# Sample keys turned by VectorE in 32x32 blocks, and scores in sixteen 32x32 tiles

## The chip, the cores and the metric

The kernel runs on one core of one Trainium2 chip. The metric is the device time of one launch in microseconds (us). The engines are TensorE (PE, with its weight loads as PEld), VectorE (DVE), ScalarE (ACT), GpSimd (POOL) and SyncE (SP); SP and POOL issue the DMAs named here.

## What is computed

Two layers of a decoder, for a prompt of 1024 tokens and for 8 sample sequences of 4 new tokens each; both share all weights. Layer 0 has a gated convolution and, beside it, differential attention. For the samples this attention reads 2048 past tokens per sequence from a paged cache: 16 pages of 128 tokens, each page a key page and a value page of 128 x 512 numbers (4 heads of 128, 256 KB in fp32), found through a page table. This is the part that the change touches:

```python
def diff_attend(q, k, v, mask, lam):
    s = jnp.einsum('bqhcd,bkhcd->bhcqk', q, k).astype(jnp.float32) * (DA_DIM ** -0.5)
    s = jnp.where(mask, s, -jnp.inf)
    p = jax.nn.softmax(s, axis=-1)
    w = p[:, :, 0] - lam * p[:, :, 1]
    return jnp.einsum('bhqk,bkhe->bqhe', w.astype(v.dtype), v)

past_k = cache_k[j, page_table].reshape(nb, -1, DA_HEADS, 2 * DA_DIM)
past_v = cache_v[j, page_table].reshape(nb, -1, DA_HEADS, 2 * DA_DIM)
keys = jnp.concatenate([past_k, k_rows], axis=1).reshape(b, p + s, DA_HEADS, 2, DA_DIM)
mask = jnp.arange(p + s)[None, :] <= (p + jnp.arange(s))[:, None]
attn = diff_attend(q, keys, vals, mask, lam)
```

The scores sum over the 64 numbers of a half head, so a key page has to stand with these numbers on the partitions, while it arrives from memory with the tokens on the partitions.

## The kernel before

Each engine has a program of its own, written out in order, and semaphores join them. Products of the large projections are made unit by unit: a unit is 24 fp16 matmuls of 128 x 352 into one PSUM bank (L372), then ACT or DVE copies the bank out. Three units share a weight tile (a visit); ACT and DVE split each weight tile into a high and a low fp16 half (L329, L345).

The attention heads of the prompt run first (`dve_head`, `pe_head`), and the units of the projection fill TensorE between their steps. In head 3 DVE also builds the sample queries: `dve_queries` clears row 19 of `arena` and makes 16 small copies, so that `q_blk` holds for each head and each sequence 32 columns, most of them zero.

Then comes the sample stage, in two rounds of four sequences. A round has four parts:

- keys: 64 key pages in 32 steps of two pages. TensorE turns both pages (8 transposes of 128 x 128, L1941) into banks 4 and 5, ACT copies bank 4 and DVE bank 5 to `kt` (L2010, L2070), and one step later TensorE makes the scores of these pages (`scores`, four matmuls of 128 x 32 by 256 columns, one for each head, side by side in the four 32-column strips of the array, L1929). The scores lie in banks 0 to 3. DVE takes the maximum of a bank as soon as it is full (`bank_max`, L2065);
- middle: the scores of the samples' own new tokens (L1952), the exponentials by ACT (L2016), their sums, and the weights turned and combined (L1958, L1960, L1965);
- values: 64 value pages in 32 steps of two (L1980), weights times values into bank 6;
- end: norm and copy-out of the result.

Both kinds of page pass through a ring of 16 pages in `hT` (`ring`). `load_page` (L1876) issues page f when page f - 16 has been used (`page_used`); SP issues two pages, then POOL the next two. The SP program also issues the weight tiles of the units (`sp_proj0`).

The order between sample work and units is written out: `woven` takes one step of the sample stage and then so many half units (12 matmuls) as ROUND_FILL has at this place. Before, it has none in the 32 key steps, two after each of the four middle steps, one in every second value step (15), and three in the end part: 26 half units a round, which is 13 units. DVE and ACT follow the same list; the second of a unit's two places is where the engine that copies the unit out waits for it. From the second convolution head on, all units use PSUM bank 7, so a unit starts when the one before it has been copied out. The units of a visit come in the order gate (copied by ACT, L1513), input (DVE, L1572) and output gate (DVE, L1591); with the first unit of the last kind DVE also makes the three convolution taps (L1538 to L1545).

After head 3 DVE still copies `v_own` (L2049), for which it waits until POOL has stored the prompt's keys and values.

Of the kernel before, what the change touches and what calls it, by code (L numbers as in the profile page):

```python
# [78 lines left out]
def build(nc, x_p, x_s, cache_k, cache_v, state_conv, state_C, state_n, state_m, page_table, norms, w_in0,  # L79
# [3 lines left out]
    with ctx:  # L83
# [1359 lines left out]
        sm_max, sm_neg = small[:, 80:85], small[:, 85:86]  # L1443
# [5 lines left out]
        q_blk = arena[:, 19, 0:SEQ].rearrange("p (h b n) -> p h b n", h=HEADS, b=NB)  # L1449
# [4 lines left out]
        kt = [arena[:, 24 + i, 0:SEQ].rearrange("p (h n) -> p h n", h=HEADS) for i in range(2)]  # L1454
# [24 lines left out]
        kp_ev = [sem("kp_ev0"), sem("kp_ev1")]  # L1479
        kp_used = sem("kp_used")  # L1480
        own_t, max_ready, exps, comb_ready = sem("own_t"), sem("max_ready"), sem("exps"), sem("comb_ready")
        q_ready, o_zero = sem("q_ready"), sem("o_zero")
# [38 lines left out]
        def dve_proj0(dve, chain, v0, v1_):  # L1521
# [24 lines left out]
            for n in range(VISITS[v0].units[0], VISITS[v1_].units[-1] + 1):  # L1546
                v, g, x = UNITS[n].visit, UNITS[n].g, ps[:, UNITS[n].bank, :]
                h, m = (v - CXB) // 3 if v >= CXB else v // 3, v % 3
                if v >= CXB and m == 2 and g == 0:
                    chain.sync()  # L1550
                    chain.mark(dve.tensor_copy(conv_new[:, h, 0:2], conv_p_in[:, SEQ:SEQ + 2]))
                    chain.mark(dve.tensor_copy(conv_new[:, h, 2:2 + 2 * NB].rearrange("p (b t) -> p b t", b=NB),
                                               conv_s_in[:, :, 4:6]))
                    tap(h, 0)
# [258 lines left out]
        def dve_head(dve, chain, h):  # L1813
# [19 lines left out]
            if h == HEADS - 1:  # L1833
                dve_queries(dve, chain)
# [20 lines left out]
        def dve_queries(dve, chain):  # L1855

            chain.link(dve.memset(arena[:, 19, 0:SEQ], 0.0))
            for b in range(NB):
                for c in range(2):
                    n = 8 * (b % 4) + 4 * c  # L1860
                    ins = dve.tensor_copy(q_blk[64 * c:64 * c + 64, :, b, n:n + NS],
                                          qT[64 * c:64 * c + 64, :, SEQ + NS * b:SEQ + NS * b + NS])
            ins.then_inc(q_ready, 1)

        ROUND_FILL = ((0,) * 32 + (2, 2, 2, 2) + (1, 0) * 15 + (0, 0) + (1, 1, 1))
# [40 lines left out]
        def pe_samples(pe):  # L1907
# [12 lines left out]
            pe.wait_ge(q_ready, 1)  # L1920
            for r_ in range(2):
                def scores(q):

                    n, b, j = 32 * r_ + q, 4 * r_ + q // 8, q % 8
                    pe.wait_ge(kp_ev[0], n + 1)
                    pe.wait_ge(kp_ev[1], n + 1)
                    pe.wait_ge(exps, 5 * r_)
                    for h in range(HEADS):
                        ins = pe.matmul(ps[32 * h:32 * h + 32, j // 2, 256 * (j % 2):256 * (j % 2) + 256],  # L1929
                                        q_blk[:, h, b, :], kt[n % 2][:, h, :], start=(b % 4 == 0 and j % 2 == 0),  # L1930
                                        stop=(b % 4 == 3), skip_group_check=True)
                    ins.then_inc(kp_used, 1)
                if r_:
                    pe.wait_ge(os_lo, 1)
                for q in range(32):
                    for e in range(2):
                        f = 128 * r_ + 2 * q + e
                        page_ready(f)
                        pe.wait_ge(kp_ev[e], 32 * r_ + q)
                        for h in range(HEADS):  # L1940
                            ins = pe.transpose(ps[:, 4 + e, h * P:(h + 1) * P], ring[:, f % RING, h * P:(h + 1) * P],  # L1941
                                               ident[:, :])
                        ins.then_inc(page_used, 1)
                    if q:
                        scores(q - 1)
                    yield
                scores(31)
# [51 lines left out]
        def act_samples(act):  # L1999
# [5 lines left out]
            for r_ in range(2):  # L2005
                for q in range(32):
                    n = 32 * r_ + q
                    act.wait_ge(page_used, 128 * r_ + 2 * q + 1)
                    act.wait_ge(kp_used, max(n - 1, 0))
                    act.activation(kt[n % 2][:, :, 0:P], ps[:, 4, :].rearrange("p (h e) -> p h e", h=HEADS),  # L2010
                                   ACT.Copy).then_inc(kp_ev[0], 1)
# [3 lines left out]
                for j in range(4):  # L2015
                    act.activation(probs[:, 512 * j:512 * j + 512], ps[:, j, :], ACT.Exp, bias=sm_neg,  # L2016
                                   accum_out=sm_sum[:, j:j + 1]).then_inc(exps, 1)
# [26 lines left out]
        def dve_samples(dve, chain):  # L2044
# [17 lines left out]
            for r_ in range(2):  # L2062
                def bank_max(j):
                    dve.wait_ge(kp_used, 32 * r_ + 26 + 2 * j)
                    chain.mark(dve.tensor_reduce(sm_max[:, j:j + 1], ps[:, j, :], AX.X, ALU.max))  # L2065
                for q in range(32):
                    n = 32 * r_ + q
# [733 lines left out]
        def _(pool):  # L2801
# [45 lines left out]
            for h in range(HEADS):  # L2847
                for ev, src, dst, n in ((v_ev, v_nat, v_p, 2), (k_ev, k_nat, k_p, 2)):
# [250 lines left out]
```

## Time and profile before

| | us |
|---|---|
| median of 3 runs | 2697.01 |
| the runs | 2692.72 to 2698.54 |
| span of the profiled execution | 2696.3 |
| PE busy in it | 2624.9 |
| DVE busy in it | 1245.7 |
| ACT busy in it | 1026.6 |
| POOL busy in it | 447.6 |

The profiled execution's span and the median differ by 0.7 us. Times in the rows below are counted from the start of the span. A row of the timeline merges instructions of one kind that follow each other; in brackets stands how long the engine was idle before and who ended it. Four records of fp32 matmul with 32-column weights lie on each other, since they use different strips of the array, so the time of one (mean ns) is much more than the time from one to the next. An fp32 matmul has two records. A row of the windows view gives the stretch and its length, then busy time and number of instructions of PE, PEld, DVE, ACT and POOL, the granted clock, the mean busy share of the DMA engines, and GB/s.

### The profile page before, as it was taken

Reading aid. Unit: us, or ns where it says so; the run is one execution under the profiler, and the core shown is the slowest. Engines: PE = TensorE matmul, PEld = TensorE weight load, DVE = VectorE, ACT = ScalarE, POOL = GpSimd, SP = SyncE. Lnnn points to the kernel's source line nnn. Section 1 sums busy time; section 2 is a strip of 40 time slices with the busy share of each in tenths; the row PEclk is TensorE's granted clock in tenths of the full one; section 3 lists DMA queues with packets and bytes.
Section 4 is the critical chain, followed back from the end, with each engine's and each line's share of the span. In section 5 each row is a group of like instructions: output and inputs, shape, how many; then the busy total and the mean of one; then the engine's idle time right before and its main releaser. Section 6 shows DMA issues by size and latency. Waiting matters only on the chain.

```text
span 2696.3 us, 49457 instructions
## 1 busy us (share of the span) xinstructions
PE 2624.9 (97%) x20217; PEld 1876.1 (70%) x20217; DVE 1245.7 (46%) x2059; ACT 1026.6 (38%) x1896; POOL 447.6 (17%) x512
## 2 busy tenths in 40 slices
PE   8999899999999999999999999999999999999998
PEld 5666666656588768886566766667656886788765
DVE  5555533335744213444754344344477541154454
ACT  4454332224443214333443333324365431244333
POOL 4000023222033002311101020111101220123121
PEclk9999999999999999999999999999999999999999
DMA  7211269771211311125435242322411112011442
GB/s 250 63 40 42 87 220 342 239 251 50 78 64 33 81 53 59 53 76 160 119 89 89 36 118 45 102 62 88 151 52 69 63 57 62 32 64 48 134 130 97
DMA packets 257659, 266.14 MB, mean 99 GB/s; under 512 B 10668, under 2 KB 217810, under 8 KB 256796
## 3 DMA queue, kind: packets, MB, share of 16 engines
q1 hardware_dynamic: 231772, 166.10, 22.0%
q0 software_dynamic: 25088, 94.79, 10.0%
q8 instruction: 162, 2.65, 0.4%
q10 hardware_dynamic: 576, 2.10, 0.2%
q14 instruction: 61, 0.50, 0.1%
HBM read 227.45 MB, written 35.50 MB: 98 GB/s over the span
## 4 chain that ended last, share of the span: by engine, by line
PE 90%; DVE 5%; ACT 2%; issue 1%; DMA 0%; POOL 0%; SPq 0%; DVEq 0%; ACTq 0%; POOLq 0%
PE ps L372 49%; PE ps L1130 25%; PE ps L1941 2%; PE ps L1929 1%; PE ps L1627 1%; PE ps L1980 1%; PE ps L1706 1%; PE ps L2475 1%; PE ps L2455 1%; PE ps L2489 1%; PE ps L2511 1%; DVE arena L883 1%; PE ps L2498 1%; PE ps L1692 1%; DVE hT L887 1%
## 5 line engine op out<-in xcount | busy, mean ns | idle before, releaser
L372 PE MATMUL ps<-u,w_split 128*128 128x352 f16 (+1 forms) x4752 | 753.0, 315 | 9.8 <-DVE u L737 5.9
L372 PEld LDWEIGHTS ps<-u,w_split 128*128 128x128 f16 (+1 forms) x4752 | 462.7, 99 | 260.8 <-issue 20.8
L372 PE MATMUL ps<-arena,w_split 128*128 128x352 f16 x3663 | 560.7, 313 | 3.7 <-DVE w_split L345 1.5
L372 PEld LDWEIGHTS ps<-arena,w_split 128*128 128x128 f16 x3663 | 357.6, 98 | 200.7 <-issue 9.4
L1130 PE MATMUL ps<-hT,w_split 128*128 128x264 f16 x3456 | 400.6, 276 | 3.2 <-ACT arena L1170 3.2
L1130 PEld LDWEIGHTS ps<-hT,w_split 128*128 128x128 f16 x3456 | 337.8, 98 | 54.9 <-issue 2.1
L345 DVE SCALAR_TENSOR_TENSOR w_split<-w_raw,w_split 128x1024 f16<-128x1024 f32 (+2 forms) x133 | 184.5, 1389 | 296.6 <-ACT w_split L329 296.1
L1130 PE MATMUL ps<-u,w_split 128*128 128x264 f16 x2592 | 303.4, 276 | 0.0
L1130 PEld LDWEIGHTS ps<-u,w_split 128*128 128x128 f16 x2592 | 253.6, 98 | 38.3
L329 ACT ACTIVATE w_split<-w_raw 128x1024 f16<-128x1024 f32 (+2 forms) x133 | 155.5, 1171 | 135.7 <-PE ps L372 97.3
L343 DVE SCALAR_TENSOR_TENSOR w_split<-arena,w_split 128x512 f16<-128x512 f32 x126 | 85.9, 724 | 103.9 <-ACT w_split L323 103.9
L1260 POOL TENSOR_TENSOR arena<-arena 128x512 f32<-128x512 f32 x18 | 22.8, 1266 | 527.6 <-DVE w_split L343 527.6
L343 DVE SCALAR_TENSOR_TENSOR w_split<-w_raw,w_split 128x512 f16<-128x512 f32 x126 | 80.9, 687 | 62.4 <-ACT w_split L323 62.4
L372 PE MATMUL ps<-arena 128*128 128x352 f16 x657 | 102.7, 316 | 0.0
L2325 ACT ACTIVATE arena<-ps 128x352 f32<-128x352 f32 x66 | 30.5, 464 | 179.7 <-PE ps L372 179.7
L817 POOL TENSOR_TENSOR arena<-arena 128x352 f32<-128x352 f32 x53 | 71.6, 1351 | 159.9 <-ACT arena L805 159.8
L1203 DVE TENSOR_TENSOR arena<-ps,arena 128x528 f32<-128x528 f32 x36 | 25.5, 707 | 153.4 <-ACT arena L1170 153.4
L1300 ACT ACTIVATE arena<-ps 128x352 f32<-128x352 f32 x48 | 22.3, 465 | 191.3 <-PE ps L372 191.3
L372 PEld LDWEIGHTS ps<-arena 128*128 128x128 f16 x657 | 64.5, 99 | 37.1 <-issue 3.1
L1216 DVE TENSOR_TENSOR arena<-arena 128x1056 f16<-128x1056 f32 (+1 forms) x60 | 58.3, 972 | 50.4 <-ACT arena L1153 41.4
L372 PE MATMUL ps<-u,arena 128*128 128x352 f16 x504 | 77.5, 313 | 3.2 <-ACT arena L1298 2.7
L323 ACT ACTIVATE w_split<-arena 128x512 f16<-128x512 f32 x126 | 71.8, 620 | 13.7 <-PE ps L1130 10.9
(405 smaller groups left out, 2987.1 us busy)
## 6 DMA issues: line engine op xcount, KB each, us to landing
w_raw<-in_w_down SPq DMA_DIRECT2D x58, 704.0 KB, 4.7
w_raw<-in_w_in SPq DMA_DIRECT2D x56, 512.0 KB, 7.7
arena<-in_w_gu SPq DMA_DIRECT2D x18, 1024.0 KB, 5.2
w_raw<-in_w_gu SPq DMA_DIRECT2D x18, 1024.0 KB, 5.2
hT<-in_cache_k SPq DMA_DIRECT2D x64, 256.0 KB, 4.3
hT<-in_cache_k POOLq DMA_DIRECT2D x64, 256.0 KB, 4.6
hT<-in_cache_v SPq DMA_DIRECT2D x64, 256.0 KB, 5.0
hT<-in_cache_v POOLq DMA_DIRECT2D x64, 256.0 KB, 5.5
```

Of the source, the lines that this page charges most:

```text
L323: act.activation(split_of(v, 0).rearrange("p (k n) -> p k n", k=kt), raw_of(v), ACT.Copy, scale=WS).then_inc(w_hi, 1)
L329: act.activation(split_of(v, 0)[:, 0:kt * n], raw_of(v), ACT.Copy, scale=WS).then_inc(w_hi, 1)
L343: dve.scalar_tensor_tensor(lo, raw_of(v), WS, hi, ALU.mult, ALU.subtract).then_inc(w_ready, 1)
L345: dve.scalar_tensor_tensor(split_of(v, 1)[:, 0:kt * n], raw_of(v), WS, split_of(v, 0)[:, 0:kt * n], ALU.mult, ALU.subtract).then_inc(w_rea ...
L372: ins = pe.matmul(ps[0:m, bank, 0:GW], split_of(v, wp)[:, k * w + col * P:k * w + col * P + m], x[:, xp, k0 + k, cols(g)], start=(k == 0 a ...
L817: pool.tensor_tensor(sum_y, sum_y, sq_y[k % 2], ALU.add).then_inc(y_added, 1)
L883: ins = dve.scalar_tensor_tensor(h_tmp[:, k % 2, :], ybuf[:, k, cols(g)], gains[:, col:col + 1], rs[0], ALU.mult, ALU.mult)
L887: dve.tensor_tensor(h, h, h_tmp, ALU.add).then_inc(h_ready, 1)
L1130: ins = pe.matmul(ps[:, bank + s_, 0:HW], split_of(v, wp)[:, k * P:(k + 1) * P], x, start=(name in ("M1", "M2", "M5") and k == 0 and q == ...
L1216: dve.tensor_tensor(hi_lo[:, 1], x, hi_lo[:, 0], ALU.subtract).then_inc(hid_ready, 1)
L1941: ins = pe.transpose(ps[:, 4 + e, h * P:(h + 1) * P], ring[:, f % RING, h * P:(h + 1) * P], ident[:, :])
L2325: act.activation((q_of[h % 2], k1, v1, o1)[m // 2][:, m % 2, cols(g)], ps[:, UNITS[n].bank, 0:GW], ACT.Sigmoid if m >= 6 else ACT.Copy, sc ...
```

## The change

- TensorE no longer turns key pages. DVE turns them where they lie in the ring, two pages (128 x 1024) with one instruction, in blocks of 32 x 32 (`dve.transpose`), and signals `page_turned`. Block (i, j) of a page keeps its place and is transposed inside, so each 32-partition strip holds 32 tokens, and the numbers of a head stand on the partitions only in runs of 32.
- The scores of four pages are made in one step, by 64 matmuls on 32 x 32 tiles: four row strips i, four heads h, and four turns s. For turn s the queries must lie rotated by 32 s partitions, so there are four copies of `q_blk`, in rows 10, 12, 13 and 14 of `arena`. Strip i writes bank i.
- These copies are made by POOL (`pool_queries`), before it stores head 3's keys and values: it clears one row, makes the 16 small copies, and issues six DMAs for the three rotated copies. `dve_queries` is gone from DVE's program, and DVE waits for the copies ahead of the third visit of the first convolution head.
- ACT no longer copies turned pages, and its exponentials write the probabilities of a bank in runs of 32. DVE no longer copies turned pages; one maximum over four banks (2048 columns) takes the place of the four of 512.
- The key pages are given back to the ring four at a time, after their scores.
- ROUND_FILL: 8 half units in the key steps (one after every fourth), 8 in the middle, 7 in the value steps (at every fourth), 3 at the end; 26 as before.

```diff
-        q_blk = arena[:, 19, 0:SEQ].rearrange("p (h b n) -> p h b n", h=HEADS, b=NB)
+        Q_ROWS = (10, 12, 13, 14)
+        q_turned = [arena[:, row, 0:SEQ].rearrange("p (h b n) -> p h b n", h=HEADS, b=NB) for row in Q_ROWS]
+        q_blk = q_turned[0]
...
+                    if h == 0:
+                        dve.wait_ge(q_copied, 2 * NB)
...
-            if h == HEADS - 1:
-                dve_queries(dve, chain)
...
-        def dve_queries(dve, chain):
-
-            chain.link(dve.memset(arena[:, 19, 0:SEQ], 0.0))
+        def pool_queries(pool, chain):
+
+            pool.wait_ge(s_done, 16 * (HEADS - 1))
+            drained(pool, last_unit(3 * HEADS - 3))
+            chain.link(pool.memset(arena[:, Q_ROWS[0], 0:SEQ], 0.0))
...
+            for s_ in range(1, 4):
+                cut = P - 32 * s_
+                pool.dma_start(arena[0:cut, Q_ROWS[s_], 0:SEQ], arena[32 * s_:P, Q_ROWS[0], 0:SEQ]).then_inc(q_ready, 16)
+                pool.dma_start(arena[cut:P, Q_ROWS[s_], 0:SEQ], arena[0:32 * s_, Q_ROWS[0], 0:SEQ]).then_inc(q_ready, 16)
...
-        ROUND_FILL = ((0,) * 32 + (2, 2, 2, 2) + (1, 0) * 15 + (0, 0) + (1, 1, 1))
+        ROUND_FILL = ((0, 0, 0, 1) * 8 + (2, 2, 2, 2) + (0, 1, 0, 0) * 7 + (0,) * 4 + (1, 1, 1))
...
+                    pe.wait_ge(page_turned, 32 * r_ + 2 * n + 2)
                     pe.wait_ge(exps, 5 * r_)
...
+                    f = (128 * r_ + 4 * n) % RING
+                    for s_ in range(4):
+                        for h in range(HEADS):
+                            for i in range(4):
+                                part_, e0 = slice(32 * i, 32 * i + 32), P * h + 32 * ((i + s_) % 4)
+                                ins = pe.matmul(ps[32 * h:32 * h + 32, i, P * j:P * j + P], q_turned[s_][part_, h, b, :],
+                                                ring[part_, f:f + 4, e0:e0 + 32], start=(b % 4 == 0 and j == 0 and s_ == 0),
+                                                stop=(b % 4 == 3 and s_ == 3), skip_group_check=True)
+                    ins.then_inc(page_used, 4)
+                for q in range(32):
+                    if q % 2:
+                        scores(q // 2)
+                    yield
...
                 for q in range(32):
-                    n = 32 * r_ + q
-                    dve.wait_ge(page_used, 128 * r_ + 2 * q + 2)
-                    dve.wait_ge(kp_used, max(n - 1, 0))
-                    dve.tensor_copy(kt[n % 2][:, :, P:2 * P],
-                                    ps[:, 5, :].rearrange("p (h e) -> p h e", h=HEADS)).then_inc(kp_ev[1], 1)
-                    if q in (27, 29, 31):
-                        bank_max((q - 27) // 2)
+                    f = 128 * r_ + 2 * q
+                    dve.wait_ge(page_loaded[f % RING // 2], 32 * (f // RING + 1))
+                    pages = ring[:, f % RING:f % RING + 2, :].rearrange("p r c -> p (r c)")
+                    dve.transpose(pages, pages).then_inc(page_turned, 1)
                     yield
-                bank_max(3)
                 dve.wait_ge(own_t, r_ + 1)
-                chain.link(dve.tensor_reduce(sm_max[:, 4:5], ps[:, 4, 0:TS], AX.X, ALU.max))
+                chain.mark(dve.tensor_reduce(sm_max[:, 0:1], flat(0, 4 * 512), AX.X, ALU.max))
+                chain.link(dve.tensor_reduce(sm_max[:, 1:2], ps[:, 4, 0:TS], AX.X, ALU.max))
...
             for h in range(HEADS):
+                if h == HEADS - 1:
+                    pool_queries(pool, chain)
```

## Rows read from the trace of the kernel before

**Rows 1.** The page: busy time of each engine.

```profile
PE 2624.9 (97%) x20217; PEld 1876.1 (70%) x20217; DVE 1245.7 (46%) x2059; ACT 1026.6 (38%) x1896; POOL 447.6 (17%) x512
```

**Rows 2.** Windows: keys, middle, values, twice; columns as explained above.

```profile
319.70:372.60 52.90, 52.63 (x512) 33.56 (x512) 23.93 (x35) 19.11 (x32) 16.75 (x31) 0.97 0.92 308
372.60:396.10 23.50, 21.44 (x172) 15.04 (x172) 4.52 (x12) 6.70 (x15) 0.54 (x1) 0.93 0.21 69
396.10:442.20 46.10, 45.94 (x726) 28.53 (x726) 11.80 (x21) 5.83 (x9) 15.73 (x29) 1.00 0.96 339
...
449.40:501.10 51.70, 51.10 (x513) 32.37 (x511) 24.46 (x36) 20.29 (x33) 16.69 (x31) 1.00 0.92 316
501.10:522.30 21.20, 19.83 (x172) 14.05 (x171) 10.17 (x24) 5.71 (x15) 0.54 (x1) 1.00 0.20 64
522.30:568.40 46.10, 45.95 (x726) 28.53 (x726) 11.27 (x20) 5.33 (x8) 12.96 (x24) 1.00 0.89 309
```

**Rows 3.** Timeline of PE, one key step (L1941 then L1929).

```profile
323.94 1.09 PE L1941 MATMUL ps<-ident,hT 128*128 128x128 f32 x8
324.97 0.64 PE L1929 MATMUL ps<-arena 128*32 128x256 f32 x8
325.54 1.09 PE L1941 MATMUL ps<-ident,hT 128*128 128x128 f32 x8
```

**Rows 4.** Timeline of PE in the value steps: a half unit, then four pages.

```profile
411.69 1.96 PE L372 MATMUL ps<-u,w_split 128*128 128x352 f16 x12
413.58 1.06 PE L1980 MATMUL ps<-hT,arena 128*4 128x128 f32 x32
414.57 0.32 PE L372 MATMUL ps<-u,w_split 128*128 128x352 f16 x1
```

**Rows 5.** Timeline of PE: two row strips of 64, and one column strip after another.

```profile
62.80 0.49 PE L1627 MATMUL ps<-arena 64*128 64x128 f32 x4
372.98 0.90 PE L1952 MATMUL ps<-arena 128*32 128x32 f32 x32
373.81 3.75 PE L372 MATMUL ps<-u,w_split 128*128 128x352 f16 x24
```

**Rows 6.** Timeline of DVE at the taps: instructions of 1024 columns, back to back.

```profile
402.50 0.75 DVE L1538 TENSOR_SCALAR arena<-arena,gains 128x1024 f32<-128x1024 f32 x1
403.43 1.23 DVE L345 SCALAR_TENSOR_TENSOR w_split<-w_raw,w_split 128x1024 f16<-128x1024 f32 x1
404.57 1.28 DVE L1541 SCALAR_TENSOR_TENSOR arena<-arena,gains 128x1024 f32<-128x1024 f32 x1
405.77 0.24 DVE L1542 SCALAR_TENSOR_TENSOR arena<-arena,gains 128x32 f32<-128x32 f32 x1
```

**Rows 7.** Timeline of DVE, the queries in head 3, and what follows them.

```profile
251.22 0.91 DVE L1857 MEMSET arena<- 128x1024 f32 x1 [0.16 <-issue]
252.16 2.91 DVE L1861 COPY arena<-arena 64x16 f32<-64x16 f32 x16
255.10 0.75 DVE L1810 SCALAR_TENSOR_TENSOR arena<-ps,gains,arena 128x512 f16<-128x512 f32 x1
```

**Rows 8.** Timeline of PE at the same place, and a later wait.

```profile
256.00 1.09 PE L1641 MATMUL ps<-ident,arena 128*128 128x128 f32 x4 [3.41 <-DVE arena L1810]
...
383.36 0.30 PE L1958 MATMUL ps<-arena 128*32 128x64 f32 x2 [1.41 <-DVE arena L2084]
```

**Rows 9.** Windows after these two waits (columns as in Rows 2).

```profile
255.00:262.00 7.00, 6.00 (x20) 3.02 (x20) 1.57 (x3) 0.69 (x1) 0.00 (x0) 0.51 0.00 0
384.80:388.20 3.40, 3.40 (x16) 2.40 (x15) 0.34 (x1) 1.54 (x2) 0.00 (x0) 0.51 0.00 0
```

**Rows 10.** Windows: value steps where the DMAs move much.

```profile
432.00:444.00 12.00, 12.00 (x192) 7.48 (x184) 1.31 (x2) 3.09 (x12) 4.46 (x9) 1.00 1.04 385
```

**Rows 11.** Timeline of DVE at the end of the first key part.

```profile
372.77 0.69 DVE L2065 TENSOR_REDUCE small<-ps 128x1 f32<-128x512 f32 x1 [0.20 <-PE ps L1929]
390.87 0.53 DVE L1572 SCALAR_TENSOR_TENSOR arena<-ps,arena 128x352 f32<-128x352 f32 x1 [1.69 <-PE ps L372]
```

More of the change, by code:

```diff
@@ L1442, in build @@
         zx, zy, zz = (small[:, 56 + 8 * i:64 + 8 * i] for i in range(3))
-        sm_max, sm_neg = small[:, 80:85], small[:, 85:86]
+        sm_max, sm_neg = small[:, 80:82], small[:, 85:86]
         sm_sum, sm_scale = small[:, 86:91], small[:, 91:92]
@@ L1453, in build @@
         comb = arena[:, 23, 64:128]
-        kt = [arena[:, 24 + i, 0:SEQ].rearrange("p (h n) -> p h n", h=HEADS) for i in range(2)]
         o_sb = arena[:, 26, 0:CH].rearrange("p (b e) -> p b e", b=4)
@@ L1478, in build @@
         ids_loaded = sem("ids_loaded")
-        kp_ev = [sem("kp_ev0"), sem("kp_ev1")]
-        kp_used = sem("kp_used")
+        page_turned = sem("page_turned")
         own_t, max_ready, exps, comb_ready = sem("own_t"), sem("max_ready"), sem("exps"), sem("comb_ready")
-        q_ready, o_zero = sem("q_ready"), sem("o_zero")
+        q_copied, q_ready, o_zero = sem("q_copied"), sem("q_ready"), sem("o_zero")
         wt_t, wt_dve, wt_act = sem("wt_t"), sem("wt_dve"), sem("wt_act")
@@ L1860, in dve_queries @@
                     n = 8 * (b % 4) + 4 * c
-                    ins = dve.tensor_copy(q_blk[64 * c:64 * c + 64, :, b, n:n + NS],
-                                          qT[64 * c:64 * c + 64, :, SEQ + NS * b:SEQ + NS * b + NS])
-            ins.then_inc(q_ready, 1)
-        ROUND_FILL = ((0,) * 32 + (2, 2, 2, 2) + (1, 0) * 15 + (0, 0) + (1, 1, 1))
+                    pool.tensor_copy(q_blk[64 * c:64 * c + 64, :, b, n:n + NS],
+                                     qT[64 * c:64 * c + 64, :, SEQ + NS * b:SEQ + NS * b + NS]).then_inc(q_copied, 1)
+            pool.wait_ge(q_copied, 2 * NB)
+            for s_ in range(1, 4):
[3 more added lines that the diff above has]
+        ROUND_FILL = ((0, 0, 0, 1) * 8 + (2, 2, 2, 2) + (0, 1, 0, 0) * 7 + (0,) * 4 + (1, 1, 1))
         SAMPLE_FILL = (1, 1, 0) + ROUND_FILL * 2
@@ L1919, in pe_samples, with scores @@
             pe.wait_ge(at_lo, 2 * HEADS)
-            pe.wait_ge(q_ready, 1)
+            pe.wait_ge(q_ready, 96)
             for r_ in range(2):
[L1922 to L1926, printed above, removed]
+                def scores(n):
+                    b, j = 4 * r_ + n // 4, n % 4
+                    pe.wait_ge(page_turned, 32 * r_ + 2 * n + 2)
                     pe.wait_ge(exps, 5 * r_)
[L1928 to L1932, printed above, removed]
+                    f = (128 * r_ + 4 * n) % RING
[11 more added lines that the diff above has]
+                    yield
@@ L1933, in pe_samples @@
                 if r_:
                     pe.wait_ge(os_lo, 1)
[L1935 to L1946, printed above, removed]
@@ L1947, in pe_samples @@
-                scores(31)
                 pe.matmul(ps[:, 4, 0:TS], smask[:, r_, :], ident[0:TS, 0:TS], start=True, stop=False,
@@ L2006, in act_samples @@
                 for q in range(32):
-                    n = 32 * r_ + q
[L2008 to L2011, printed above, removed]
                     yield
@@ L2014, in act_samples @@
                 act.wait_ge(max_ready, r_ + 1)
-                for j in range(4):
-                    act.activation(probs[:, 512 * j:512 * j + 512], ps[:, j, :], ACT.Exp, bias=sm_neg,
-                                   accum_out=sm_sum[:, j:j + 1]).then_inc(exps, 1)
+                for i in range(4):
+                    act.activation(probs[:, 0:2 * SEQ].rearrange("p (f i t) -> p i f t", i=4, t=32)[:, i],
+                                   ps[:, i, :].rearrange("p (f t) -> p f t", t=32), ACT.Exp, bias=sm_neg,
+                                   accum_out=sm_sum[:, i:i + 1]).then_inc(exps, 1)
                 act.activation(probs[:, 2 * SEQ:2 * SEQ + TS], ps[:, 4, 0:TS], ACT.Exp, bias=sm_neg,
```

4 lines of the change are left out of this document (removed).

## The prediction, made before the changed kernel was run

> **What bounds the kernel now.** I read the page first: TensorE is busy for 97% of the span, DVE for 46% [rows 1]. So a change pays only where it takes time from TensorE, or where TensorE waits. Next I cut the sample stage into its parts with the windows view [rows 2]: keys 52.9 and 51.7 us, middle 23.5 and 21.2, values 46.1 twice. In every key and value part PE is busy nearly all the time; DVE is below half. So TensorE's order of work sets the length of these parts, and the DMAs (308 to 339 GB/s) follow it. Third, the timeline of PE gives prices. A key step is 1.60 us: 1.03 for the turning, 0.57 for the scores [rows 3], 32 of them 51 us. A half unit is 1.89 us, and four value pages are 0.99 us [rows 4]. The values' 32 steps and 15 half units are thus 8 x 1.98 + 15 x 1.89 = 44 us, which is the 46.1 of the row but for the own tokens.
>
> **TensorE's part of the change.** Out go 512 transposes: 64 steps x 1.03 = 66 us. The old scores (64 x 0.57 = 36 us) give way to 32 calls of 64 matmuls, 128 records each. No row shows a 32 x 32 tile. From below: the call for four value pages streams 128 columns in 32 records, four column strips at once, and takes 0.99 us [rows 4]. The new call has as many columns a record and four times the records; if the row strips overlap like the column strips, it takes the same 0.99 us. That row strips do overlap is seen in the prompt's scores: four records on two strips of 64 rows take 0.49 us [rows 5], one pair after another. From above: 32 records that follow each other in one column strip at a time take 0.83 us until the next line begins [rows 5], 26 ns each; 128 of them 3.3 us, which also is about what the call costs if only the columns overlap (4 x 0.99 less the changeovers, 3.4). I take 1.0 us, the row with the same moving size, and keep 3.3 for the range. TensorE's own work in a key part is then 16 x 1.0 + 8 x 1.89 = 31 us, and in a value part 16 + 7 x 1.89 = 29 us. So TensorE is late in neither; what is late next decides.
>
> The Trainium skill (TensorE: Matmul & The Clock Gate, Part 3) gives for sixteen 32 x 32 tiles a speedup of 10.6 and a span of one matmul plus about 4 ns for each further tile. The rows above agree with the side by side running of four tiles; of sixteen no run here shows it yet. By that rule the call would be near my 1.0 us too.
>
> **Key parts: DVE is late.** DVE now has 32 turnings in each. The nearest rows are DVE instructions over 1024 fp32 columns in SBUF: 0.75 us for the cheapest form, 1.23 and 1.28 for the others, which begin 1.14 and 1.20 us apart [rows 6]. A turning has to pass each element through once, and I take 1.18 us apart. The bounds are 0.67 (the cheap form, back to back) and, since nothing here shows how 4-byte elements are turned, twice my value, 2.36.
> DVE also follows ROUND_FILL. At every second fill place it waits for the unit of TensorE, and behind this wait the next turnings are queued; TensorE waits for them. When DVE has turned the eighth pair, TensorE still needs one call (1.0) and a half unit (1.89) before the unit is ready, then DVE copies it out (0.53 [rows 11]): 3.4 us in which nothing is turned. This doesn't happen where ACT copies the unit out.
> - Round one has units of the gate (two, ACT) and of the input (two, DVE): 32 x 1.18 + 2 x 3.4 = 44.6. In the stretches without a stop DVE would use 16 pages in 9.4 us, which is 4.19 MB or 446 GB/s; the row with much traffic shows 385 [rows 10], so about 1.5 us are added. 46 us against 52.9.
> - Round two has four DVE units, one of them with the taps: 37.8 + 4 x 3.4, and 1.0 for the first tap and 1.4 for the part of split and taps (1.2 + 3.1) that is longer than TensorE's 2.9, and 0.7 before the first turning: 54.5 us against 51.7.
> Together -4 us; a turning of 1.28 makes it +2, one of 1.05 -12. The gain of 66 us on TensorE is nearly all lost to this chain.
>
> **Clock.** The stops leave TensorE idle for some 2.5 to 3 us each, six of them or more. After a wait of 3.41 us, and after one of 1.41 us [rows 8], the granted clock was 0.51 for 7.0 and for 3.4 us [rows 9], which is the 1.2 GHz level. Each such stretch of 3.4 us costs 1.7 us of TensorE's work, and about half of it lies on the path. I put +5 us; the bounds are 0 and, with the low clock all through both key parts, +20.
>
> **Middle.** The maximum over 2048 columns can start only behind the last scores: four times 0.6 against one bank's 0.69 [rows 11], +1.8 us ahead of the exponentials, for which TensorE already waited 1.41 us [rows 8]. The taps of the first round move here, 4 us on DVE, while all units share bank 7: +2. In round two one of these is hidden. +4 us together (0 to 7).
>
> **Values.** 15 half units become 7, so TensorE needs 29 us. But 48 of the 64 pages are still to be loaded when the part begins, 12.6 MB: at 385 GB/s [rows 10] 32.7 us, and with some 3 us until the first lands, 0.6 MB of weights, and SP's pages held behind a weight tile that waits for a split, 38 us. From 46.1, twice: -16 us (bounds -24, where the DMAs go faster than any row shows, and -10).
>
> **Head 3.** `dve_queries` held DVE for 3.9 us [rows 7]; TensorE waited 3.41 us for the L1810 behind it, and then ran 7 us at clock 0.51 [rows 8, 9]. Both go: without them L1810 starts near 251.5, and TensorE's half unit still lasts until 252.6. -6 us (-3.4 to -6.8). On POOL the same work takes some 4 us and the six DMA issues 5 us ahead of head 3's stores, which are waited for only some 60 us later (`v_own`), so it costs nothing; if POOL were 60 us late, the whole would be added. The wait on `q_copied` is over long before.
>
> **Sum.** -6 (head 3) - 4 (keys) + 5 (clock) + 4 (middle) - 16 (values) = -17 us. The profiled execution's 2696.3 and the median 2697.0 differ by 0.7, so it stands for either: 2680 us.
>
> **Rivals.**
> 1. *Slower, TensorE's tiles.* If the row strips don't overlap, a call is 3.3 us; 16 pages take 4 x 3.3 + 2 x 1.89 = 17 us, a key part 70 instead of 52. Twice 70 against 104.6 is +35, which takes the place of the keys' -4 and the clock's +5; with -6, +4 and -16 that is +17, about 2714. It decides from a call of about 2.2 us. For it: 32-row tiles are in no row, and dispatch of 256 instructions a call might bind. Against: [rows 4, 5].
> 2. *Slower, the turning costs twice.* At 2.36 us the keys take 64 x 1.18 = 75 us more, -17 + 75 = +58, of which the clock's and the DMA's terms give back some: about 2750. The break-even is 1.18 + 17/64 = 1.45 us.
> 3. *The gain is absorbed.* With the low clock through most of the key parts, and values bound nearer the 339 GB/s of the whole part: -6 - 4 + 15 + 4 - 10 = -1, about 2695. The same comes out where the change doesn't do what it says, because TensorE's freed time is idle time.
>
> For rival 2 the Trainium skill has two statements. VectorE: DVE Perf Modes, The three transpose paths, gives 311 ns for a 128 x 128 turning in bf16; an estimate from it, eight times that for 1024 columns, is 2.5 us. The Vector Engine (DVE) Microarchitecture Reference, section 3.8, says one element per cycle and lane, and an estimate from that is about 1.1 us. No run here shows either yet; the first would give rival 2's time, the second mine.
>
> **How the numbers follow.** Forecast 62% (its own range 2658 to 2693), absorbed 14%, rival 1 12%, rival 2 8%, other 4%. The range 2660 to 2716 leaves out rival 2 and a few per cent at each end. A difference of 0.2% (5.4 us) is about what a measurement can tell from no change. Faster by more than that: nearly all of the forecast and a little of the absorbed, 0.62; within: 0.16; slower: rivals 1 and 2 and some others, 0.22.
>
> **What would show it.** The turnings' mean in the list of groups: 1.15 to 1.25 us. The call's 128 records in the timeline of PE: near 1.0 us. Key parts of 46 and 54 us with idle gaps of PE put down to DVE's turnings, and granted clock below 1 in them; value parts near 38 us with DMA at 380 GB/s; no gap at 253 us. I am wrong if a turning takes over 1.45 us, a call over 2.2 us, or the value parts stay at 46 us.

## The result, and the profile of the changed kernel

The changed kernel takes 2745.9 us (median of 4 runs, 2745.2 to 2750.2) against 2697.6 for the one before on the same chip: a ratio of 1.019, with a 95% interval of 1.018 to 1.020. It is slower, outside the predicted range and on the other side of no change. The profiled execution has a span of 2743.6 us, 47.3 more than before.

The page of the changed kernel, busy time of each engine and the shares of the chain that ended last:

```profile
PE 2604.1 (95%) x23289; PEld 1869.5 (68%) x23289; DVE 1269.6 (46%) x2036; ACT 987.7 (36%) x1832; POOL 454.3 (17%) x535
...
PE 87%; DVE 5%; issue 3%; ACT 2%; DMA 2%; SPq 0%; POOL 0%; DVEq 0%; ACTq 0%; POOLq 0%
```

TensorE is busy for 21 us less than in [rows 1], so it now stands idle for longer by far more than that. The windows of the sample stage, with the columns and in the order of [rows 2] (keys, middle, values, twice):

```profile
313.00:398.40 85.40, 57.14 (x2146) 38.88 (x2145) 39.75 (x36) 3.84 (x5) 17.23 (x32) 0.84 0.66 205
398.40:422.55 24.15, 21.33 (x166) 14.52 (x165) 12.19 (x25) 5.59 (x14) 0.00 (x0) 0.93 0.14 47
422.55:463.85 41.30, 32.99 (x630) 20.70 (x629) 3.50 (x5) 3.78 (x6) 16.08 (x30) 0.95 0.99 355
...
472.00:556.46 84.46, 55.29 (x2145) 38.41 (x2145) 44.17 (x48) 2.05 (x3) 16.64 (x31) 0.84 0.63 202
556.46:579.90 23.44, 21.38 (x167) 14.85 (x169) 7.49 (x14) 8.60 (x18) 0.54 (x1) 0.93 0.19 59
579.90:621.46 41.56, 34.40 (x630) 21.42 (x629) 7.80 (x15) 1.55 (x2) 12.88 (x24) 0.92 0.94 329
```

The loss is in one place. Against [rows 2] the stage begins 6.7 us earlier (head 3); the key parts are longer by 32.5 and 32.8 us; the middles by 0.7 and 2.2; the values are shorter by 4.8 and 4.5; what lies between the rounds is 0.9 longer; all behind the stage is 5.8 shorter. -6.7 + 65.3 + 2.9 - 9.3 + 0.9 - 5.8 = 47.3. (The first cut is at the first key step. By the last instruction of head 3 the stage begins 4.8 us earlier and the first key part is 30.5 longer.) In the first key part no resource is full: PE is busy for 67%, DVE for 47%, the DMAs move 205 GB/s where they moved 308. But PE and PEld have four times the records: 2146 and 2145 for 512 and 512.

The groups with the most busy time between 315 and 640 us (busy, mean ns | idle before them and what ended it), and what TensorE does in the middle of the first key part:

```profile
L1937 PE MATMUL ps<-hT,arena 32*32 32x128 f32 x4096 | 74.9, 322 | 55.6 <-issue 36.3 <-DVE hT L2062 19.2
L2062 DVE STREAM_TRANSPOSE hT<-hT 128x1024 f32<-128x1024 f32 x64 | 74.0, 1213 | 17.3 <-DMA hT<-in_cache_k 17.2
...
L1979 PE MATMUL ps<-hT,arena 128*4 128x128 f32 x1024 | 36.0, 280 | 15.5 <-DMA hT<-in_cache_v 12.9 <-issue 2.3
...
L2065 DVE TENSOR_REDUCE small<-ps 128x1 f32<-128x2048 f32 x2 | 4.6, 2290 | 1.3 <-PE ps L1951 1.3
```

```profile
326.50 1.96 PE L1937 MATMUL ps<-hT,arena 32*32 32x128 f32 x128 [0.51 <-issue]
331.29 1.32 PE L1937 MATMUL ps<-hT,arena 32*32 32x128 f32 x77 [2.83 <-issue]
332.55 1.96 PE L372 MATMUL ps<-u,w_split 128*128 128x352 f16 x12
334.44 2.92 PE L1937 MATMUL ps<-hT,arena 32*32 32x128 f32 x166
339.78 1.89 PE L1937 MATMUL ps<-hT,arena 32*32 32x128 f32 x90 [2.42 <-issue]
```

Two things are to be seen. A call, 128 records, takes 1.9 to 2.0 us where nothing disturbs it, not 1.0. And two thirds of the idle time ahead of the calls is "issue": it has no releaser. The second timeline shows such gaps of 2.4 to 2.8 us ahead of 77 and of 90 records, which is in the middle of a call, where the code has no wait. So it looks as if TensorE is short of instructions there. The DMA queues of the second key part of after, and then of before:

```profile
q1 hardware_dynamic: 5647, 8.90, 33.6%
q0 software_dynamic: 2400, 7.87, 27.6%
q8 instruction: 17, 0.28, 1.3%
```

```profile
q1 hardware_dynamic: 4546, 8.28, 47.1%
q0 software_dynamic: 2425, 7.95, 44.1%
q8 instruction: 4, 0.07, 0.5%
```

In the first key part of after these blocks start 3.8 to 8.0 us apart (median 4.5), in the second 5.0; 17 in 85 us. In the whole trace of before no two are less than 5.4 us apart.

The trace ties the gaps to these packets. After has 23 gaps of TensorE over 0.3 us put down to "issue" in the two key parts, 37.9 us together. Every one of them ends 1.2 to 1.5 us after a packet of q8 has landed. Within a key part, from one such gap to the next TensorE makes 127 or 128 matmul records, or a multiple of that, which with as many weight loads is one block of 256. So a gap moves through the calls as the half units shift the block's edge (77, then 90, 104 and 117 records of a call behind it); it isn't bound to a place in the code.

The Trainium skill (Runtime: NRT & Kernel Launch, Instruction fetch mechanics) says that an engine's instructions are refilled in 16 KiB blocks of 256 over a queue of its own, which the trace agrees with, and that crossing a block is mostly hidden because dispatch is slower than the fill. In the key parts of this kernel the second doesn't hold: a call executes in 1.9 us and the next block comes 4.5 us after the one before.

### The profile page after: what moved, and what is told of

Same layout as the page of the kernel before. It is cut to its first block, busy times and chain, and to the rows that moved or that the text cites. A ratio compares the mean times of both kernels' runs of the same rounds, so it can differ in the third digit from the quotient of the medians.

```text
span 2743.6 us, 55251 instructions
## 1 busy us (share of the span) xinstructions
PE 2604.1 (95%) x23289; PEld 1869.5 (68%) x23289; DVE 1269.6 (46%) x2036; ACT 987.7 (36%) x1832; POOL 454.3 (17%) x535
## 4 chain that ended last, share of the span: by engine, by line
PE 87%; DVE 5%; issue 3%; ACT 2%; DMA 2%; SPq 0%; POOL 0%; DVEq 0%; ACTq 0%; POOLq 0%
PE ps L372 48%; PE ps L1130 24%; PE ps L1937 3%; PE ps L1629 1%; DMA hT<-in_cache_v 1%; PE ps L1708 1%; PE ps L2464 1%; PE ps L2444 1%; PE ps L2478 1%; PE ps L1979 1%; PE ps L2500 1%; PE ps L2487 1%; PE ps L1694 1%; DVE arena L897 1%; PE ps L2528 1%
## 5 line engine op out<-in xcount | busy, mean ns | idle before, releaser
L372 PE MATMUL ps<-u,w_split 128*128 128x352 f16 (+1 forms) x4752 | 765.8, 318 | 12.8 <-DVE u L737 5.9
L1937 PE MATMUL ps<-hT,arena 32*32 32x128 f32 x4096 | 74.9, 322 | 55.6 <-issue 36.3
L1937 PEld LDWEIGHTS ps<-hT,arena 32*32 32x32 f32 x4096 | 57.3, 113 | 73.0 <-issue 49.9
L2314 ACT ACTIVATE arena<-ps 128x352 f32<-128x352 f32 x66 | 30.5, 463 | 179.8 <-PE ps L372 179.7
L2062 DVE STREAM_TRANSPOSE hT<-hT 128x1024 f32<-128x1024 f32 x64 | 74.0, 1213 | 17.3 <-DMA hT<-in_cache_k 17.2
```

The costliest lines, as they stand in the source:

```text
L372: ins = pe.matmul(ps[0:m, bank, 0:GW], split_of(v, wp)[:, k * w + col * P:k * w + col * P + m], x[:, xp, k0 + k, cols(g)], start=(k == 0 a ...
L1937: ins = pe.matmul(ps[32 * h:32 * h + 32, i, P * j:P * j + P], q_turned[s_][part_, h, b, :], ring[part_, f:f + 4, e0:e0 + 32], start=(b % 4 ...
L2062: dve.transpose(pages, pages).then_inc(page_turned, 1)
L2314: act.activation((q_of[h % 2], k1, v1, o1)[m // 2][:, m % 2, cols(g)], ps[:, UNITS[n].bank, 0:GW], ACT.Sigmoid if m >= 6 else ACT.Copy, sc ...
```

## The experiments

**Theory A** is that the rate at which TensorE gets instructions sets the key parts. Its rivals, with the letters of the expectations: B, pages that come late; C, the streaming of columns in TensorE, or tiles that don't overlap. Beside these stand the fill order and the low clock. "K" is the time to the first instruction behind the scores, in round one from the end of head 3's last one, in round two from the start of round one's last transposes (L1995 before, L1994 after). "V" is the time from the first to the last matmul of the value steps. Before: K 54.8 and 54.0, V 45.6 twice. After: K 85.3 and 86.9, V 40.4 and 41.0. Where no number of runs stands, a variant ran once, while the runs of one kernel lie up to 9 us apart (before: 2690.1 to 2698.8). So K and V, which lie in the stage itself, decide more than the totals.

### Fewer turns of the queries, and narrow ones

```
-                    for s_ in range(4):
+                    for s_ in range(1):
...
-                                                stop=(b % 4 == 3 and s_ == 3), skip_group_check=True)
+                                                stop=(b % 4 == 3 and s_ == 0), skip_group_check=True)
```

> The changed kernel with one of the four turns of each scores call left out of none but the first: three of four turns are left out (their part of the sample scores is missing), so a call has 16 matmuls, 64 instructions, in place of 256. Pages, turnings, half units are as before. Theory A (TensorE is short of instructions: in the key parts it gets one block of 256 instructions in about 4.6 us, and each call uses one block): 16 x 64 + 192 = 1216 instructions a key part, 4.75 blocks, 22 us, so the supply no longer binds, and DVE's turnings and its stops do: key parts of 45 and 51 us in place of 85.4 and 84.5, total near 2670 us, no idle of TensorE put down to issue. Theory B (pages come back to the ring late, four at a time, and DVE waits for them): key parts stay above 70 us, since the release of the pages is the same but for 1.3 us a call; total above 2715.

The same with `range(3)` and `s_ == 2`:

> The changed kernel with one of the four turns of each scores call left out (a quarter of the sums of the sample scores is missing): 192 instructions a call. Theory A (instruction supply): 16 x 192 + 192 = 3264 instructions, 12.75 blocks of 4.6 us = 59 us a key part, total near 2692 us. Theory C (the calls are long because sixteen tiles run slower than I had it, 0.44 us a turn in place of 0.25, and TensorE is the bound): 16 x 0.44 = 7 us less a key part, total near 2730.

And with all four turns, three of which stream a quarter of the columns:

```
+                                k = 1 if s_ else 4
+                                ins = pe.matmul(ps[32 * h:32 * h + 32, i, P * j:P * j + 32 * k], q_turned[s_][part_, h, b, :],
+                                                ring[part_, f:f + k, e0:e0 + 32],
```

> The changed kernel with all 64 matmuls of a call, but in three of the four turns only 32 of the 128 columns are streamed (the sample scores lack the rest). The number of instructions is the same. Theory A (instruction supply): key parts stay at 80 to 85 us, total 2735 to 2745. Theory C (streaming in the tiles binds): a call falls from 1.8 to about 0.9 us and the key parts by 14 us each, total near 2715.

Measured, beside 2694.4 for the kernel before:

| | us | K | blocks in the first K, median us apart |
|---|---|---|---|
| one turn | 2682.2 | 52.0, 56.0 | 5, 10.9 |
| three turns | 2710.3 | 68.0, 68.4 | 13, 5.1 |
| four, three of them narrow | 2745.0 | 81.6, 84.0 | 17, 4.5 |
| after | 2745.9 | 85.3, 86.9 | 17, 4.5 |

The groups of the first key part with one turn, and then with narrow ones:

```profile
L2062 DVE STREAM_TRANSPOSE hT<-hT 128x1024 f32<-128x1024 f32 x32 | 37.2, 1215 | 8.0 <-DMA hT<-in_cache_k 8.0
...
L1937 PE MATMUL ps<-hT,arena 32*32 32x128 f32 x512 | 9.8, 339 | 20.3 <-DVE hT L2062 20.3
```

```profile
L2063 DVE STREAM_TRANSPOSE hT<-hT 128x1024 f32<-128x1024 f32 x32 | 37.2, 1215 | 14.5 <-DMA hT<-in_cache_k 14.5
L1938 PE MATMUL ps<-hT,arena 32*32 32x32 f32 (+1 forms) x2048 | 27.3, 243 | 31.2 <-issue 23.7 <-DVE hT L2063 7.5
```

With a quarter of the instructions the "issue" is gone and TensorE waits for DVE's turnings, as the prediction had it everywhere. With narrow turns the streamed columns fall by 56% (128 to an average of 56 a record), an undisturbed call from 1.9 to 1.50 us, PE's busy time with them, and the key parts only by 3 to 4 us: the time goes into "issue" (23.7 us in this key part, 20.4 in that of after). That is against C. (Their total hides it: the two K are 6.6 us shorter together, the values 2.5 longer, and the part behind the stage 6.0 longer, of which more below.) Two sizes missed: one turn gave 2682, not 2670, with DVE waiting 8.0 us for pages in the first key part; three turns gave 2710, not 2692, with blocks 5.1 us apart, not 4.6.

### The pages' traffic taken away

The second of these has 2 in place of 32.

```
-            eng.dma_start(ring[:, f % RING, :], cache[0, ds(page, 1), :, :, :].rearrange("a t h e -> (a t) (h e)")
+            w = 32 if f // 64 % 2 == 0 and f >= RING else P
+            eng.dma_start(ring[0:w, f % RING, :], cache[0, ds(page, 1), 0:w, :, :].rearrange("a t h e -> (a t) (h e)")
```

> The changed kernel, but from the seventeenth page on a key page is loaded only in its first 32 of 128 tokens (64 KB in place of 256; the other tokens keep what the ring held, so the sample scores are of other keys). Instructions and turnings are the same. Theory B (late pages): DVE's waits for pages go, key parts fall towards 50 to 60 us, total near 2690. Theory A with a supply that doesn't depend on the other DMA traffic: no change, 2735 to 2745. Theory A with fetches that queue behind page packets: the block's 4.6 us shrink towards the call's own 1.9 plus some, key parts of 60 to 70, total near 2710, and the idle of TensorE put down to issue shrinks by more than half.

> The changed kernel, but from the seventeenth page on a key page is loaded in 2 of 128 tokens only (4 KB; the rest keeps old content, so the sample scores are of other keys). In the key parts the DMAs then carry nearly nothing but weights and instructions. If the 4.5 us between two instruction blocks are a latency of the fetch itself, they stay near 4 us and the key parts at 70 to 80 us, total 2725 to 2740. If they are queueing behind page packets, they fall to the call's own 2 us or so, key parts near 55, total near 2690. With a quarter of the traffic the spacing was 3.9 and 4.3 us.

A quarter of the keys' bytes gave 2733.5 us, K 74.8 and 81.1, blocks 3.9 and 4.3 apart. This lay between the theories (fetch latency, or contention of q8 with the pages), so the second kernel left 2 of 128 tokens: 2727.0 us, K 74.2 and 80.5, blocks 3.8 us apart in both. The first key part of that kernel:

```profile
DMA packets 4535, 5.23 MB, mean 71 GB/s; under 512 B 1020, under 2 KB 3068, under 8 KB 4515
...
q8 instruction: 17, 0.28, 1.6%
```

The 71 GB/s are a mean with the value pages at the end of the part. In the stretch from 322 to 352 us the DMAs move 10 GB/s (columns of the first line: stretch, length, PE's busy time and records, clock, DMA share, GB/s):

```profile
322.00:352.00 30.00, 24.69 (x1121) 1.00 0.05 10
...
q8 instruction: 9, 0.15, 1.9%
```

Even there the blocks start 3.3 to 3.9 us apart, where a call takes 1.9, and the part is still 19 us longer than before the change. So page traffic adds about 0.7 to 1.2 us a block to the median, and the rest is there without it. This also answers B: with nearly no page traffic K falls by only 11 and 6 us.

The trace shows what a block's time is made of. The packet takes 1.0 us (median, in every kernel). From its landing to TensorE's first instruction behind a gap it is 1.2 to 1.5 us, in after as here. From there to the start of the next packet it is 1.2 us here and 2.2 in after (medians); this is where the page traffic shows. Why these three follow each other and don't overlap isn't seen.

### The order of the tiles

```
-                        for h in range(HEADS):
-                            for i in range(4):
+                        for i in range(4):
+                            for h in range(HEADS):
```

> The changed kernel with the two inner loops of a scores call exchanged: for each turn the row strip is now outside and the head (column strip) inside. Same matmuls, same number. In the changed kernel a turn takes 0.44 us in place of the 0.25 that I took from the value pages. If the order of the tiles causes this (a tile's second record held behind its first, and the tiles of one column strip in a row), an undisturbed call of 128 records falls from 1.9 to about 1.1 us in the timeline. If the number of tiles or the loads of weights set it, it stays at 1.9. In both cases the instruction supply keeps the total within 5 us of 2744.

2755.8 us, K 83.4 and 89.3; an undisturbed call still 1.96 us. The total missed its band by 7 us, but not in the key parts, which are 0.5 us longer together: the values are 3.4 longer and the part behind the stage 6.4. So neither the time of a call nor the supply comes from which strip of the array changes first.

### Half the instructions for the same work: eight pages a call

```
-                    b, j = 4 * r_ + n // 4, n % 4
-                    pe.wait_ge(page_turned, 32 * r_ + 2 * n + 2)
+                    b, j = 4 * r_ + n // 2, n % 2
+                    pe.wait_ge(page_turned, 32 * r_ + 4 * n + 4)
...
-                                                ring[part_, f:f + 4, e0:e0 + 32],
+                                                ring[part_, f:f + 8, e0:e0 + 32],
...
-                    ins.then_inc(page_used, 4)
+                    ins.then_inc(page_used, 8)
...
-                    if q % 2:
-                        scores(q // 2)
+                    if q % 4 == 3:
+                        scores(q // 4)
```

> The changed kernel with scores of eight pages in one call (256 columns streamed in place of 128, calls at every fourth step, eight pages given back at once): the whole result is computed with half as many score matmuls. Theory A (instruction supply): 8 x 256 + 192 = 2240 instructions, 8.75 blocks of 4.6 us = 40 us a key part, so it no longer binds; DVE's stops or the half-empty ring do, at 50 to 58 us; total 2680 to 2700. Theory C (streaming): the same columns, no change, 2744. Theory B (late pages): eight at a time makes it worse, above 2750.

2714.2 us (median of 4), ratio to before 1.008 (1.006 to 1.009); K 65.7 and 70.9 with 8 and 9 blocks. The groups of the first key part:

```profile
L2062 DVE STREAM_TRANSPOSE hT<-hT 128x1024 f32<-128x1024 f32 x32 | 37.6, 1219 | 15.3 <-DMA hT<-in_cache_k 15.2
...
L1937 PE MATMUL ps<-hT,arena 32*32 32x256 f32 x1024 | 27.8, 484 | 21.6 <-DVE hT L2062 21.6
```

The "issue" ahead of the calls is gone and 18 us of the 32 a part come back, with the same result computed and the same columns streamed. I had expected 2680 to 2700 and key parts of 50 to 58. What is left is another limit: TensorE takes pages in eights and gives them back in eights, DVE waits 15.2 us for pages and TensorE 21.6 for DVE. In this fill the half unit and DVE's copy of it lie at the place where DVE should turn ahead, so I moved it:

```
-        ROUND_FILL = ((0, 0, 0, 1) * 8 + (2, 2, 2, 2) + (0, 1, 0, 0) * 7 + (0,) * 4 + (1, 1, 1))
+        ROUND_FILL = ((0, 0, 1, 0) * 8 + (2, 2, 2, 2) + (0, 1, 0, 0) * 7 + (0,) * 4 + (1, 1, 1))
```

> The kernel with eight pages a call (whole result), and the half units of the key steps placed after every third step of four, ahead of the call instead of behind it. VectorE's stop at a unit then has no call in it: TensorE makes the half unit while VectorE turns. With eight pages a call the key parts were 65.7 and 70.9 us, bound by VectorE waiting for pages and units. I expect 58 to 62 each and a total near 2700, still not below the kernel before (2694), since eight pages returned at once leave VectorE waiting for loads. If the stops were not the cause, no change from 2714.

2709.8 us (median of 4), ratio 1.006 (1.004 to 1.008), K 64.4 and 70.8. I had expected 58 to 62 and about 2700. The total is 4 us lower, with intervals that overlap, the key parts are 1.4 us shorter together, and DVE's wait for pages grew from 15.2 to 19.1 us. So the stops at the units weren't what bound; the circle of pages, eight at a time in a ring of 16, is the likely limit, though no run here changes it alone.

### The old fill, and the value pages

> The changed kernel with the old ROUND_FILL: no half units in the key steps, 15 in the value steps. Theory A (instruction supply): 16 blocks of 4.6 us = 74 us a key part in place of 85, value parts 46 in place of 41.4: total about 2744 - 22 + 9 = 2731. If DVE's stops at the units are what makes the key parts long: 16 x 1.8 + stops gone, key parts of 40 to 50, total near 2685.

2727.4 us, K 72.6 and 72.3, V 45.6 twice, as before the change. With no half units in the key parts, TensorE runs them at the 1.2 GHz level:

```profile
333.77 2.81 PE L1937 MATMUL ps<-hT,arena 32*32 32x128 f32 x127 [1.04 <-issue]
337.87 2.81 PE L1937 MATMUL ps<-hT,arena 32*32 32x128 f32 x128 [1.29 <-issue]
```

A call takes 2.81 us in place of 1.9, and the gap shrinks by about as much: the blocks stay 4.4 us apart (4.43 and 4.31). In this stage 126 us run at the low level, 75 in after and 7 before, and it costs little where the supply is the bound. The part is shorter than in after by 12.7 us: there are 16 blocks' worth of instructions, not 17 (4.5 us), and TensorE's and DVE's stops for the units are gone, a share that no run here separates. If DVE's stops were what made the key parts long, they should have come to 40 to 50 us. What the new fill gained in V (10 us) it lost in K (27).

> The changed kernel, but a value page is loaded only in its first 32 of 128 tokens (the sample values are wrong in the rest). Tests what binds the value parts, 41.3 and 41.6 us in the changed kernel: if the page DMAs do, as I predicted (38), they fall to TensorE's own 30 to 32 us and the total by about 20 us to 2725. If TensorE or its clock binds, they stay above 38.

The edit is the one above with `f // 64 % 2 == 1` and 32. 2724.5 us, V 33.9 and 33.1, where after has 40.4 and 41.0: the loads of the value pages bind there. With a quarter of their bytes TensorE is busy for 89% and 94% of the two parts:

```profile
416.61:450.78 34.17, 30.46 (x625) 20.13 (x628) 3.50 (x5) 3.78 (x6) 13.56 (x27) 1.00 0.50 134
564.21:597.60 33.39, 31.26 (x625) 20.98 (x628) 7.78 (x15) 1.55 (x2) 11.93 (x24) 0.95 0.47 126
```

That the total met 2725 is partly luck: the values gave 14 us of the 20, and the key parts, from which this edit also takes traffic, 11.

### The queries alone

The kernel before, with `dve_queries` replaced by the same zeroing and copies on POOL (`pool_queries`, one copy of the queries, no DMAs) and DVE's wait on `q_copied`.

> The kernel before with only the sample queries moved from DVE to POOL (into row 10, no rotated copies); all else is as before. My prediction's term for head 3: the 3.41 us wait of TensorE at 253 us goes and with it the stretch at half clock, -6 us, 2691; -3 if the clock falls elsewhere. If the low clock merely moves, 2694 to 2697.

2687.8 us (median of 9) against 2694.4 (median of 13), ratio 0.997 (0.996 to 0.998): -6.6 us where 6 were forecast, and faster than both kernels. Windows of this kernel around the place of [rows 8] (columns as in [rows 2]):

```profile
245.00:255.00 10.00, 9.62 (x68) 6.27 (x66) 6.69 (x14) 4.18 (x8) 2.61 (x4) 1.00 0.61 170
255.00:262.00 7.00, 7.00 (x50) 4.57 (x49) 3.47 (x9) 5.63 (x16) 0.00 (x0) 1.00 0.01 2
```

The wait and the 0.51 clock of [rows 9] are gone, and the sample stage is as before (K 54.8 and 54.0, V 45.6): the profiled spans are 2690.2 against 2696.3, with 5.1 us won ahead of the sample stage and 0.9 behind it.

## Why the prediction was wrong, point by point

- **The price of a call.** This is the step that failed. I set 64 matmuls at 1.0 us from [rows 4], because a record there streams as many columns, with bounds of 1.0 and 3.3. An undisturbed call takes 1.9: a turn of 32 records costs 0.51 us alone and about 0.47 for each of three more, and the order doesn't explain it (1.96 us), the width only in part (1.50 us with 56% of the columns gone). The Trainium skill's span of one matmul and about 4 ns for each further tile (TensorE: Matmul & The Clock Gate, Part 3), which by the prediction's estimate would have put it near 1.0, isn't met here: the trace has 1.9. But that alone is inside my bounds and below rival 1's 2.2 us. What made it 4.5 to 5 is the block of 256 instructions that each call needs and waits for, which I had priced at nothing. "TensorE is late in neither" was wrong by it. I counted records (four times as many) and never asked what brings them; [rows 2] had the number, 512 in 52.9 us, and the DMA view of that stretch has 4 blocks, 13 us each. In rival 1 I had "dispatch of 256 instructions a call might bind" as an aside without a price.
- **Rival 1** gives the right sign by another mechanism: the strips do overlap (128 records in 1.9 us, 15 ns each, against 26 in its upper bound). Its 2714 was still 32 short.
- **The turning.** Forecast 1.18 us apart, bounds 0.67 and 2.36. The mean is 1.21 us, and the timeline of DVE shows eight in a row in 9.12 us, 1.14 each:

```profile
314.51 9.12 DVE L2062 STREAM_TRANSPOSE hT<-hT 128x1024 f32<-128x1024 f32 x8
```

  Right, and rival 2 falls. The Trainium skill's 311 ns for a 128 x 128 turning in bf16 (VectorE: DVE Perf Modes, The three transpose paths), taken eight times, gave the estimate of 2.5 us, which is not what this size and type cost. The estimate of about 1.1 us from the skill's one element per cycle and lane (the Trainium skill, Vector Engine (DVE) Microarchitecture Reference, section 3.8) agrees with the 1.14.
- **DVE's chain in the keys.** With one turn, where the supply is no bound, the key parts came out at 52.0 and 56.0 by K, that is 2.8 shorter and 2.0 longer than before. I had -6.9 and +2.8, before the clock's term. The first fell short mainly by DVE's 8.0 us of waits for pages. I had them at 1.5, which is the price for one ring of 16 pages, and the sum takes it once although 48 pages are loaded in the part. TensorE does wait for DVE's turnings there (20.3 us), so the stops were right in kind. They are in after too, though hidden under the larger loss:

```profile
516.87 0.52 DVE L1593 SCALAR_TENSOR_TENSOR arena<-ps,arena 128x352 f32<-128x352 f32 x1 [9.25 <-PE ps L372]
517.31 9.12 DVE L2062 STREAM_TRANSPOSE hT<-hT 128x1024 f32<-128x1024 f32 x8
...
535.69 0.52 DVE L1593 SCALAR_TENSOR_TENSOR arena<-ps,arena 128x352 f32<-128x352 f32 x1 [8.86 <-PE ps L372]
```

- **Clock.** I expected stretches below full clock and put +5. There are 75 us of them in the stage, and the clock is 0.84 in the key parts. What they cost of the 47 isn't separated; the old fill shows that in a part bound by supply more of it costs nothing visible.
- **Middle.** +4 forecast, +2.9 measured. The maximum over 2048 columns took 2.29 us, 2.4 forecast.
- **Values.** -16 forecast, -9.3 measured. The bound was named rightly (loads, not TensorE: 12.9 us of idle ahead of L1979 put down to them, and V falls to 33.1 and 33.9 with a quarter of the bytes). The rate was mis-sized: 355 and 329 GB/s in these windows, not the 385 of [rows 10], which was a stretch of 12 us.
- **Head 3.** -6 forecast, bounds -3.4 and -6.8. The last step of head 3 begins 6.3 us earlier and ends 4.8 earlier; by itself on the kernel before, the edit brings 5.1 ahead of the sample stage. Right.
- **Behind the stage** I had nothing; 5.8 us came off. Before had four stretches of 3.4 us at the low clock there (at 579, 678, 1293 and 1463 us) that after doesn't have. This doesn't come with the change: the variants with narrow turns and with the other order of tiles have the same four stretches as before, and take 2128.4 and 2128.8 us from the last value matmul to the end, as before with 2128.1; after and the other variants of it take 2122 to 2126. So it varies from one execution or variant to another, and no part of it is to be counted for the change.
- **The sum.** The kernel with one turn has all the parts of the change but three quarters of the score matmuls, and so not the supply's load. It took 2682.2 us, where the forecast was 2680.0; against the one run of the kernel before beside it (2694.4) that is -12, not -17. Its keys came to -0.8 where keys and clock together had +1, its middles to +2.8 (forecast +4), head 3 to -5.0 (-6). What the values' -9.0 lacked (-16) was made up in good part by 4.4 us behind the stage, which is luck. The other 63.7 us to after come with the three further turns.

**Open** is why a turn of 32 records takes 0.47 us more and not the 0.25 of the forecast, why a block takes 3.3 to 3.9 us with next to no traffic, when its packet takes 1.0, and why the block rate was 5.1 and not 4.5 with three turns. The old fill with eight pages a call wasn't tried.

## What to carry to other kernels

Count the instructions of a stretch, not only their busy time: divide PE's and PEld's records by 256 for the blocks of instructions, and if they must come faster than any two do in the trace of before (here 5.4 us), give them a price. Each block then costs its own time and not the time of its instructions: here 4.5 to 5 us against 1.9. Small tiles save columns and multiply instructions; with twice the columns a record, and half the records, the supply no longer bound here. When an engine's idle time is "issue", in the middle of a loop body without a wait, look at the instruction queue among the DMAs: do the gaps lie a block of 256 instructions apart, and do they end just after a packet lands?

## What the runs showed of the hardware that was not expected

- TensorE's instructions came at one block of 256 in 4.5 to 5 us beside page traffic of 200 GB/s, 3.8 us with nearly no key pages to load (3.3 to 3.9 in a stretch at 10 GB/s). At the 1.2 GHz level, beside page traffic, it was 4.4 us. That is about 13 to 20 ns an instruction, while each block's packet itself takes 1.0 us. In after and in the run with the least traffic TensorE went on 1.2 to 1.5 us after a packet had landed.
- Sixteen 32 x 32 fp32 tiles over 128 columns: 0.51 us for one turn of 32 records, 1.9 for four, 2.81 at the 1.2 GHz level; over 256 columns 2.76 for four turns. So wider tiles are cheaper: 1.38 us for four pages in place of 1.9.
- VectorE turns 128 x 1024 fp32 in place in 32 x 32 blocks in 1.21 us, 1.14 each in a row, the distance at which the 1.23 us instructions of [rows 6] begin.
